# ScalarE's order in the head loop of a decoder trunk: the first head's scaling ahead of the second key tile, and the casts of the gate units in odd steps

## What is computed

```python
def token_mixer(x, ...):
    hn = rms_norm(x, attn_norm)
    qa, ka, va, cq, ckv, kr, gates = jnp.split(hn @ w_in, SPLIT_IDX, axis=-1)
    ...                                   # branch A: q, k of 8 heads x 64, norm, partial rotary
    ya = moba_attention(qa, ka, va)       # with 256 tokens: causal softmax attention
    qb = heads(rms_norm(cq, cq_norm) @ w_uq, B_HEADS)       # branch B, low rank
    kv = heads(rms_norm(ckv, ckv_norm) @ w_ukv, B_HEADS)
    ...
    yb = causal_attention(qb, kb, vb)     # softmax(q k^T * scale + mask) @ v, 8 heads
    g_a, g_b = jnp.split(gates, 2, axis=-1)
    merged = jax.nn.sigmoid(g_a) * (ya @ w_br_a) + jax.nn.sigmoid(g_b) * (yb @ w_br_b)
    return merged @ w_out
def reference(x, ...):
    for l in range(DEPTH):
        x = x + token_mixer(x, ...)
        h = rms_norm(x, ffn_norm[l])
        x = x + (swiglu(h, ...) if l % 2 == 0 else moe_swiglu(h, ...))
    return x
```

## Time and profile before

| | |
|---|---|
| time, median of 3 runs | 1229.38 us (1229.37 to 1231.62) |
| time of the profiled execution | 1233.2 us |
| its span, first to last instruction | 1231.4 us |
| TensorE busy | 1195.9 us, 97% of the span |
| VectorE busy | 445.9 us, 36% |
| ScalarE busy | 381.3 us, 31% |
| head loop of the first layer | from 77 us to 148 us |
| head loop of the second layer | from 447 us to 518 us |
| experts | from 572 us to the end |

### The profile page before, as it was taken

How to read it: one execution, slowest core, us unless ns; L and a number is a source line. 1 busy time by engine, 2 the same in 40 slices (tenths; PEclk the granted TensorE clock), 3 DMA queues, 4 the chain that set the end, 5 groups by cost and what they waited for, 6 DMA issues and landing times.

```text
span 1231.4 us, 27855 instructions
## 1 busy us (share of the span) xinstructions
PE 1195.9 (97%) x12520; PEld 802.7 (65%) x12520; DVE 445.9 (36%) x756; ACT 381.3 (31%) x640; POOL 71.8 (6%) x85
## 2 busy tenths in 40 slices
PE   9999999999999999999999999999997999999976
PEld 7877788888889877787566645644553445445533
DVE  4776665644446676665111101210211012101001
ACT  6698846443337598842000000000000000000000
POOL 0520000000001420000000000000000000000000
PEclk9999999999999999999999999999999999999999
DMA  8643544755445643579999999999999999999993
GB/s 277 222 137 104 171 171 140 239 201 175 150 157 190 212 136 103 172 260 419 425 422 423 421 422 420 423 422 422 423 423 420 423 420 423 423 420 423 423 423 144
DMA packets 73775, 376.31 MB, mean 306 GB/s; under 512 B 7370, under 2 KB 11124, under 8 KB 49076
## 3 DMA queue, kind: packets, MB, share of 16 engines
q1 hardware_dynamic: 72416, 371.04, 77.0%
q0 software_dynamic: 864, 2.36, 0.5%
q10 hardware_dynamic: 372, 1.07, 0.2%
HBM read 372.35 MB, written 2.10 MB: 304 GB/s over the span
## 4 chain that ended last, share of the span: by engine, by line
PE 84%; DMA 12%; ACT 2%; SPq 1%; DVE 1%; issue 1%; DVEq 0%; ACTq 0%
PE ps L1274 26%; PE ps L1307 13%; PE ps L780 12%; PE ps L782 12%; PE ps L781 12%; DMA m_unit<-in_experts_dram 8%; DMA s_unit<-in_experts_dram 3%; PE ps L1290 1%; PE ps L912 1%; PE ps L965 1%; SPq L716 1%; PE ps L905 1%; PE ps L901 1%; PE ps L938 1%; ACT w_hi L1420 1%
## 5 line engine op out<-in xcount | busy, mean ns | idle before, releaser
L1274 PE MATMUL ps<-s_unit,eT 128*32 128x352 f32 x3936 | 300.7, 459 | 5.6 <-DMA s_unit<-in_experts_dram 5.6
L1274 PEld LDWEIGHTS ps<-s_unit,eT 128*32 128x32 f32 x3936 | 138.3, 110 | 155.4 <-issue 111.7
L1763 DVE TENSOR_TENSOR w_lo<-raw,w_hi 128x2048 fp32r<-128x2048 f32 (+3 forms) x93 | 197.1, 2125 | 110.9 <-ACT w_hi L1420 110.3
L1420 ACT CAST w_hi<-raw 128x2048 fp32r<-128x2048 f32 (+3 forms) x93 | 165.5, 1783 | 120.1 <-PE ps L782 105.3
L780 PE MATMUL ps<-w_hi,hT_hi 128*128 128x512 f32 (+1 forms) x464 | 179.8, 387 | 1.7 <-DVE w_lo L2039 0.9
L782 PE MATMUL ps<-w_hi,hT_lo 128*128 128x512 f32 (+1 forms) x464 | 176.5, 380 | 0.0
L781 PE MATMUL ps<-w_lo,hT_hi 128*128 128x512 f32 (+1 forms) x464 | 175.9, 379 | 0.0
L1708 ACT ACTIVATE e_act<-ps 128x352 f32<-128x352 f32 x42 | 19.5, 463 | 500.1 <-PE ps L1274 500.1
L1307 PE MATMUL ps<-s_unit,hidT 128*32 128x256 f32 x1936 | 119.0, 383 | 3.7 <-DMA s_unit<-in_experts_dram 3.7
L1274 PE MATMUL ps<-m_unit,eT 128*32 128x352 f32 x1440 | 110.8, 459 | 5.6 <-DMA m_unit<-in_experts_dram 5.5
L2187 DVE TENSOR_TENSOR e_act<-e_act,ps 128x352 f32<-128x352 f32 x42 | 21.2, 504 | 258.0 <-ACT e_act L1708 256.9
(11 more groups left out here) (221 smaller groups left out, 1159.2 us busy)
## 6 DMA issues: line engine op xcount, KB each, us to landing
s_unit<-in_experts_dram SPq DMA_DIRECT2D x128, 1408.0 KB, 30.8
m_unit<-in_experts_dram SPq DMA_DIRECT2D x64, 1408.0 KB
raw<-in_w_in_dram SPq DMA_DIRECT2D x28, 1024.0 KB, 5.4
raw<-in_dense_w_gate_up_dram SPq DMA_DIRECT2D x20, 1024.0 KB, 5.2
raw<-in_dense_w_down_dram SPq DMA_DIRECT2D x9, 1024.0 KB, 4.9
raw<-in_w_out_dram SPq DMA_DIRECT2D x8, 1024.0 KB, 4.9
raw<-in_w_in_dram SPq DMA_DIRECT2D x8, 672.0 KB, 4.6
raw<-in_w_branch_a_dram SPq DMA_DIRECT2D x4, 1024.0 KB, 5.0
```

Source lines behind the costliest of these rows:

```text
L1274: last = pe.matmul(ps[2 * g + gu][strip(q), 0:PIECE], eT[:, g, STRIP * b:STRIP * (b + 1)], unit[:, at:at + PIECE], start=b == 0, stop=b == ...
L1420: act.copy(w_hi[u % SPLIT][:, 0:SIZE[u]], raw[u % RAW][:, 0:SIZE[u]]).then_inc(hi_ready, 1)
L1763: dve.tensor_tensor(w_lo[q][:, 0:m], raw[u % RAW][:, 0:m], w_hi[q][:, 0:m].bitcast(F32), ALU.subtract).then_inc(split, 1)
```

## The change

Two things move in ScalarE's program, in both layers; no instruction is added or removed, and the programs of TensorE, VectorE, GpSimd and SyncE stay the same. `scale_probs(0)` goes ahead of `kv_out(1)`. And the casts of units u0+16 to u0+23 move from the even steps 0, 2, ..., 14 to the odd steps 1, 3, ..., 15, each one step later; within its step a cast still stands behind the scaling and the copies.

```diff
                 kv_out(0)
                 exponentials(0)
+                scale_probs(0)
                 kv_out(1)
-                scale_probs(0)
                 exponentials(1)
...
                     copy_out(pT[:, k % 2, :], t_, ps[t_.bank][:, 0:3 * P])
-                    if k == 0:
-                        hi(u0 + 16)
-                    elif k + 1 in ON_ACT:
+                    if k and k + 1 in ON_ACT:
                         scale_probs(k + 1)
...
                         copy_out(qkT_b[0:B_DIM, hd, :], t_, ps[t_.bank][0:B_DIM, :])
-                    if k and k % 2 == 0:
+                    if k % 2:
                         hi(u0 + 16 + k // 2)
                     if k and k % 4 == 0:
                         turned_y(l, k // 4 - 1)
```

## The result

The changed kernel took 1237.01 us, the median of six executions (1235.6 to 1239.6); the kernel before took 1230.3 us beside it (six, 1229.37 to 1231.62). The ratio is 1.0051, with a 95% interval from 1.0039 to 1.0063: slower by about 6.3 us (the two medians lie 6.7 apart), where 6.2 were forecast. The profiled execution took 1235.92 us with a span of 1234.1.

A forecast was written before the change was run, and what follows sets the result against it. TensorE, busy 97% of the span, was taken as the bound, with head-loop delays moving the whole DMA-fed expert stage. Two layers by 3.1 us gave 6.2, added to 1229.4: 1235.6 us, range 1232.0 to 1238.5.

The forecast's parts named there:

- The start: gain 0.65, loss 0.36.: Start of the head loop: head 0's transposes stop waiting 0.65 us, head 1's wait 1.0, TensorE ends late by 0.36.
- Cast 16 leaves step 0: nothing.: Before exp(2): the cast had filled an idle stretch, so ScalarE idles about 2.2 us and the 0.70 wait stays.
- Cast 16 goes to step 1: a new wait.: exp(3) late by 2.16 us; values matmuls of heads 2 and 3 wait 1.34, TensorE late by 1.70.
- Steps 3 to 6.: Rotary piece costs about 0.1 us, the 0.93 wait at heads 4 and 5 goes; head 6's transposes late by 1.87.
- The middle.: Heads 6 to 12: no new stall above some 0.2 us, the 0.26 wait goes, TensorE late by 1.61.
- The end of the loop: a second new wait.: Head 15: inv(15) queues behind split 22, which waits for cast 22; TensorE waits 1.5 us, late by 3.1.
- The sum.: Two layers lose 3.1 us each, 6.2 together, added to the median of 1229.4: 1235.6 us.
- fifth rival: More stalls in the middle, a cast behind a late scale, 1 us a layer more: 1237.6, up to 1238.5; 12%.
- A rule weighed.: Head loop: an idle TensorE could drop from 2.4 to 1.2 GHz; the forecast expected granted clock 1.00 and no clock cost.
- the covered end: Rival: idle time in the middle brings exp(13) back, only 1.6 us a layer stay, 1232.6; 14%.
- The faster one: Rival: odd-step casts fit ScalarE's idle time if exp(3)'s delay stays under 0.56 us; 4.4 gained, 1225.0; 6%.
- The expert stage absorbed nothing: Answers the no-change rival: the expert stage takes its length from the DMA queues and absorbs the delay, 1229.4; 6%.

## Why the prediction was right

Its sign held, its time lies within the stated range (1235.6 for 1237.01 measured), and its mechanism held, with some terms too small. The list of waits that it read has three more rows outside the expert stage, 1.2, 0.9 and 0.8 us; they lie in the first 60 us, are the same in the changed kernel and change nothing in the argument. The steps by their names, "late by" measured from L882:

- **The start: gain 0.65, loss 0.36.** Head 0 waits no more, head 1 waits 0.99 (forecast 1.0), and TensorE is late by 0.35. In the second layer 0.63 of the 1.35 at head 0 stays and 0.97 comes at head 1. The scaling alone lost the same 0.33 and 0.38.
- **Cast 16 leaves step 0: nothing.** ScalarE idles 2.08 there (forecast about 2.2), and the wait of heads 0/1 stays, 0.72.
- **Cast 16 goes to step 1: a new wait.** VectorE waits 2.45 for exp(3), forecast 2.4; the values of heads 2/3 wait 1.32, forecast 1.34; late by 1.75, forecast 1.70. Cast 16 alone brings this stall and nothing else.
- **Steps 3 to 6.** The wait of 0.93 went as said, but the term of 0.1 for the rotary piece was mis-sized. TensorE is late by 1.91 at the first transposes of the second branch and by 2.27 at those of head 5, so 0.16 and 0.36 came in place of 0.1. The second of these I had not named: VectorE's maximum (L1851, at 99.50) empties the bank that the transposes of head 5 need, and it too stands behind the late inv(5). So TensorE is late by 1.33 at heads 4/5, not 0.87. This error did no harm: at head 6 the forecast was 1.87 and 1.90 was measured, since that time is set by split 16 on VectorE and not by TensorE's own arrival; the wait is shorter by what TensorE was already late (0.41 in the brackets, 0.57 more lateness, for 1.0). The maximum, in VectorE's timeline of the changed kernel:

```profile
99.50 0.56 DVE L1851 TENSOR_TENSOR h_scaled<-ps,cst 128x384 f32<-128x384 f32 x1 [0.21 <-DVE mix L1811]
```

- **The middle.** The 0.26 went, but TensorE got later by 0.26 around head 7 (2.18 for 1.92), where the forecast allowed some 0.2 and put it at nothing. Late by 1.86 for 1.61. No bracket shows a wait there, but the starts do. Scale(7) on ScalarE and the transposes of head 7 on TensorE, before:

```profile
105.84 0.80 ACT L1526 ACTIVATE h_scaled<-h_scaled,small 128x128 f32<-128x128 f32 x2
```

```profile
109.13 0.49 PE L912 MATMUL ps<-cst,h_scaled 128*128 128x128 f32 x3
```

and in the changed kernel:

```profile
109.54 0.81 ACT L1526 ACTIVATE h_scaled<-h_scaled,small 128x128 f32<-128x128 f32 x2
```

```profile
110.40 0.55 PE L912 MATMUL ps<-cst,h_scaled 128*128 128x128 f32 x3
```

Before, the scaling was done 2.5 us ahead of its transposes. Now it ends at 110.35 and they start 0.05 later, the hand-over that the forecast used; with all casts moved and the scaling of head 0 in its old place the gap is 0.06, with cast 16 left in step 0 it is 0.05, and with casts 18 and 20 alone the scaling is done 0.8 ahead and nothing is lost. So the likely cause is cast 18, which now stands behind the late scale(6) and ahead of exp(7). This is argued from the times; no run moved cast 18 back alone.
- **The end of the loop: a second new wait.** The transposes of head 15 wait 1.27 (forecast 1.5), behind split 22 as said; late by 3.33 for 3.1, which is the 0.25 carried over from the middle. The kernel with split 22 moved divides the 1.4 of this stall: 1.07 is the queue on VectorE, and the rest stays with exp(15) late behind cast 22.
- **The sum.** 6.67 in the traces, 6.2 forecast. The time shows 0.51% of 1230.3, or 6.3, with an interval from 4.8 to 7.8. The 1237.01 lies above the 1233.8 to 1236.8 that the forecast gave itself and nearest to the fifth rival's 1237.6: 0.9 of the 1.4 is the kernel before, which took 1230.3 beside it and not 1229.4, and 0.5 are the terms too small.
- **A rule weighed.** A window of the changed kernel (length, then busy time of each engine, clock, share and rate of the DMA queues) keeps the clock:

```profile
72.00:94.00 22.00, 19.41 (x105) 14.23 (x104) 16.41 (x37) 15.95 (x44) 6.71 (x4) 1.00 0.31 95
```

The granted clock is 1.00 there, as in the other windows of both loops, which is the 2.4 GHz level, through waits of up to 1.32. The rule of the Trainium skill ("TensorE: Matmul & The Clock Gate", part 1) on an idle array was not called on by waits of this length.

Of the rivals, the covered end fell with the 1.27 at head 15. The fifth, a cast behind a late scaling in the middle, came true in a quarter of its size, by the reading above: some 0.25 a layer and not 1. The faster one decided at copy(3), and exp(3) was late by 2.14 (87.35 for 86.05, with the 0.84 by which this trace is earlier), far over its 0.56. The expert stage absorbed nothing: its first load came 16.19 after the last values matmuls in both traces.

## What to carry to other kernels

In an engine's fixed order, put long work of low priority ahead of instructions that have a bracket: there the cast cost nothing (0.27 of waiting stayed behind the old cast 16), and the same cast in front of one without a bracket delayed it by its whole 1.8 us. Whether that costs anything is decided further on, since casts 18 and 20 in odd steps brought no new wait. So follow the queue of the engine that waits for the late instruction: most of the cost came from what stood behind inv(3) and from what stood ahead of inv(15). The second was tested by a run, the first is read from who released whom. A move that removes one wait should be priced at the next consumer too, since the scaling gave head 0 what it took from head 1; and moving two casts out of eight (0.9984) did what moving all eight (1.0043) did not, so a regular pattern is best tried one piece at a time.

## What the runs showed that was not expected

- A late instruction of VectorE also holds back TensorE through a bank: the transposes of head 5 waited 0.16 to 0.17, in both layers, for the maximum of head 6, which had not yet read its scores out of the bank that they need.
- In the second layer a load of the function table of 1.28 us stood on the path ahead of exp(0), and explains why head 0 waited 1.35 there and 0.65 in the first layer: with the load moved away it waits 0.65 there too. The Trainium skill ("ScalarE: Activation LUTs", What ACT_TABLE_LOAD costs) gives about 1283 ns for the load, which agrees, and about 1380 ns more for a drain, of which these rows show nothing: the next instruction starts at 426.07, right behind the load's end at 426.06, and on the path (441.90) the load starts 0.02 behind the end of the copies. There it cost 0.75.
- From its first load to the end of the span the expert stage, the same program in every kernel, took 694.9 to 698.2 us from trace to trace. That is 3.3 of scatter, while the start of L882 in the first layer lies between 66.5 and 68.0, and the time between the two stretches repeats to 0.02. So most of the scatter of the traces comes from the expert stage, and it is as large as most of the effects measured here. Why that stage varies no run shows.
